# Gate columns and index weights with the tokens stationary, in a float32 two-block transformer kernel on Trainium2

## The reference, cut to what matters

```python
# first block: h is (256, 1024); the last 36 columns of w_in are the gates
z = h @ w_in
a_conv, q, kc_r, vc_r, ks, vs, kw, vw, g = jnp.split(z, splits, axis=-1)
gates = jax.nn.sigmoid(g).reshape(b, t, N_KV_HEADS, Q_PER_KV, N_BRANCH)   # 12 heads x 3 branches
out = gb[..., 0:1] * o_c + gb[..., 1:2] * o_s + gb[..., 2:3] * o_w

# second block: 8 index heads, w_i is (256, 8)
qa, ka, va, qb, kb, vb, qi, ki, wi, gate_a, gate_b = jnp.split(proj, split_at, axis=-1)
rel = jax.nn.relu(jnp.einsum('bqhd,bsd->bqhs', qi, k_i))
isc = jnp.einsum('bqhs,bqh->bqs', rel, wi) * idx_scale
logit = jnp.einsum('bqhd,bqkhd->bqhk', qa, kg) * scale     # "scores a", after a top-k by isc
```

## Time and profile before

| | before |
|---|---|
| runs | 737.31, 736.04, 737.00 us |
| median of the runs | 737.0 us |
| the profiled execution's own time | 736.97 us |
| its span, first to last instruction | 735.1 us |
| mean granted TensorE clock | 0.995 |
| busy: PE, PEld | 98%, 90% of the span |
| busy: DVE, ACT, POOL | 73%, 53%, 5% of the span |

### The profile page before, as it was taken

The page is one execution under the profiler, slowest core; times in us unless marked ns, Lnnn a source line. Parts: engine busy times, 40 slices in busy tenths (PEclk is TensorE's granted clock), DMA queues, the critical chain, the costliest instruction groups (busy, mean ns, idle before and its releaser), DMA issues.

```text
span 735.1 us, 13433 instructions
## 1 busy us (share of the span) xinstructions
PE 721.5 (98%) x5430; PEld 664.1 (90%) x5430; DVE 536.3 (73%) x935; ACT 388.9 (53%) x567; POOL 37.6 (5%) x53
## 2 busy tenths in 40 slices
PE   7999999999999999999999999999999999999996
PEld 7999987799999999988999989999888899999995
DVE  6798898676767777758569979995877885455554
ACT  7655999463344433447255457676446435445442
POOL 2700000000000000000532000000000000000000
PEclk9999999999999999999999999999999999999999
DMA  9746611678888778631554447454813774554511
GB/s 328 247 135 227 225 56 59 252 308 311 323 314 323 301 290 309 229 121 57 184 182 175 173 158 300 174 200 169 319 57 115 284 264 155 212 182 169 220 58 58
DMA packets 27024, 151.12 MB, mean 206 GB/s; under 512 B 3129, under 2 KB 7837, under 8 KB 9565
## 3 DMA queue, kind: packets, MB, share of 16 engines
q1 hardware_dynamic: 22620, 124.81, 46.7%
q10 hardware_dynamic: 3456, 25.17, 8.7%
q0 software_dynamic: 896, 0.43, 0.3%
HBM read 148.92 MB, written 1.05 MB: 204 GB/s over the span
## 4 chain that ended last, share of the span: by engine, by line
PE 84%; DVE 10%; ACT 3%; issue 1%; DMA 1%; SPq 0%; DVEq 0%; ACTq 0%
PE ps L464 25%; PE ps L465 24%; PE ps L466 24%; DVE w_lo L1820 3%; PE ps L860 2%; PE ps L598 1%; PE ps L622 1%; DVE misc L2333 1%; PE ps L582 1%; PE ps L1115 1%; DVE misc L2327 1%; DVE small L2332 1%; DMA raw<-rows_b 1%; PE ps L653 1%; PE ps L635 1%
## 5 line engine op out<-in xcount | busy, mean ns | idle before, releaser
L1820 DVE TENSOR_TENSOR w_lo<-raw,w_hi 128x2048 fp32r<-128x2048 f32 (+2 forms) x105 | 237.0, 2262 | 99.3 <-ACT w_hi L1294 99.1
L464 PE MATMUL ps<-h_hi,w_hi 128*128 128x256 f32 (+2 forms) x984 | 279.8, 284 | 0.0
L465 PE MATMUL ps<-h_lo,w_hi 128*128 128x256 f32 (+2 forms) x984 | 278.3, 283 | 0.0
L466 PE MATMUL ps<-h_hi,w_lo 128*128 128x256 f32 (+2 forms) x984 | 278.3, 283 | 0.0
L1294 ACT CAST w_hi<-raw 128x2048 fp32r<-128x2048 f32 (+2 forms) x105 | 197.0, 1888 | 49.4 <-PE ps L466 45.5
L464 PEld LDWEIGHTS ps<-h_hi,w_hi 128*128 128x128 f32 (+2 forms) x984 | 187.2, 190 | 2.5 <-issue 1.3
L465 PEld LDWEIGHTS ps<-h_lo,w_hi 128*128 128x128 f32 (+2 forms) x984 | 187.2, 190 | 1.1
L466 PEld LDWEIGHTS ps<-h_hi,w_lo 128*128 128x128 f32 (+2 forms) x984 | 187.2, 190 | 0.3
L464 PE MATMUL ps<-w_hi,mix_hi 128*128 128x512 f32 x248 | 97.6, 394 | 0.6 <-DVE small L1965 0.4
L465 PE MATMUL ps<-w_lo,mix_hi 128*128 128x512 f32 x248 | 96.8, 390 | 0.0
L466 PE MATMUL ps<-w_hi,mix_lo 128*128 128x512 f32 x248 | 96.5, 389 | 0.0
(11 more groups left out here) (326 smaller groups left out, 891.3 us busy)
## 6 DMA issues: line engine op xcount, KB each, us to landing
raw<-wts SPq DMA_DIRECT2D x109, 1024.0 KB, 4.8
ada<-w_ada ACTq DMA_DIRECT2D x24, 1024.0 KB, 5.2
alibi<-wts SPq DMA_DIRECT2D x2, 1024.0 KB, 6.0
fa_whole<-wts SPq DMA_DIRECT2D x2, 1024.0 KB, 5.8
resid<-x SPq DMA_DIRECT2D x2, 512.0 KB, 3.8
raw<-wts SPq DMA_DIRECT2D x2, 512.0 KB, 6.6
rows_ga<-rows_wide SPq DMA_DIRECT2D x1, 1024.0 KB, 8.4
out<-resid SPq DMA_DIRECT2D x4, 256.0 KB, 2.0
```

What stands on the lines that cost most here:

```text
L464: nc.tensor.matmul(o, lh, rh, start=start, stop=False)
L465: nc.tensor.matmul(o, lh, rl, start=False, stop=False)
L466: return nc.tensor.matmul(o, ll, rh, start=False, stop=stop)
L1820: V.tensor_tensor(w_lo[:, s % RING, 0:w], raw[:, n_of[name] % RAW, 0:w], w_hi[:, s % RING, 0:w].bitcast(F32), ALU.subtract).then_inc(w_rea ...
```

## The change

Both narrow projections are now made with the tokens stationary and 36 or 8 weight columns moving, once for each half of the tokens, so that they come out with tokens on the partitions. The copies to `gT` and `wiT` and the four transposes go. ACT reads the result where the transposes used to leave it. And four more slices of "sg0" stand ahead of `scores_a(0)`.

```diff
-            def narrow_tile(slot, o, a, n, cols):
+            def narrow_rows(slot, o, a, n, cols):
                 wh, wl = w3(slot, DC, DC * cols)
-                for k in range(DC):
-                    i = mm3(o, wh[:, k, a:a + n], wl[:, k, a:a + n], h_hi[:, k, :], h_lo[:, k, :], k == 0, k == DC - 1)
+                for m in range(2):
+                    ms = slice(m * P, (m + 1) * P)
+                    for k in range(DC):
+                        i = mm3(o(m), h_hi[:, k, ms], h_lo[:, k, ms], wh[:, k, a:a + n], wl[:, k, a:a + n], k == 0, k == DC - 1)
                 return i
...
-                narrow_tile(slot, ps[0:G_COLS, bank, 0:T], 0, G_COLS, G_COLS).then_inc(pe_tile, 1)
+                narrow_rows(slot, lambda m: ps[:, bank, T + m * HD:T + m * HD + G_COLS], 0, G_COLS, G_COLS).then_inc(pe_tile, 1)
...
-            def gate_turn():
-
-                pe.wait_ge(narrow_sb, 1)
-                for m in range(2):
-                    i = nc.tensor.transpose(ps[:, 7, T + m * HD:T + m * HD + G_COLS], gT[:, m * P:(m + 1) * P], ident[0:G_COLS, 0:G_COLS])
-                i.then_inc(narrow_ps, 1)
...
             cmp_values()
-            gate_turn()
             pe.wait_ge(lnv_ready, 1)
...
-            narrow_tile(slot, ps[0:NB_HEADS, bank, T:2 * T], P, NB_HEADS, IDX_COLS).then_inc(pe_tile, 1)
+            narrow_rows(slot, lambda m: ps[:, 7, m * NB_HEADS:(m + 1) * NB_HEADS], P, NB_HEADS, IDX_COLS).then_inc(pe_tile, 1)
...
             feature_2("qi0")
-            pe.wait_ge(narrow_sb, 2)
-            for m in range(2):
-                i = nc.tensor.transpose(ps[:, 7, m * NB_HEADS:(m + 1) * NB_HEADS], wiT[:, m * P:(m + 1) * P], ident[0:NB_HEADS, 0:NB_HEADS])
-            i.then_inc(narrow_ps, 1)
             feature_2("qi1")
...
-            gate_half(0, 0, 0, 3)
+            gate_half(0, 0, 0, 7)
             scores_a(0)
-            gate_half(0, 0, 3)
+            gate_half(0, 0, 7)
             gate_half(0, 1)
...
-                elif name == "g":
-                    nc.scalar.copy(gT, ps[0:G_COLS, bank, 0:T]).then_inc(narrow_sb, 1)
...
-                act.wait_ge(narrow_ps, 1)
+                act.wait_ge(pe_tile, s_idx["g"] + 1)
                 nc.scalar.activation(gates, ps[:, 7, T:T + 2 * HD] ... ACT.Sigmoid).then_inc(z_evac, 1)
...
-            copy_out(s_idx["g"])
             cmp_silu(1)
...
                 if name == "idx":
-                    nc.scalar.copy(wiT, ps[0:NB_HEADS, bank, T:2 * T]).then_inc(narrow_sb, 1)
+                    nc.scalar.copy(wi_s, ps[:, 7, 0:2 * NB_HEADS].rearrange("p (m h) -> p m h", m=2)).then_inc(wi_ready, 1)
                     nc.scalar.copy(kiT, ps[:, bank, 0:T]).then_inc(z_evac, 1)
...
-                if name == "qi0":
-                    act.wait_ge(narrow_ps, 2)
-                    nc.scalar.copy(wi_s, ps[:, 7, 0:2 * NB_HEADS].rearrange("p (m h) -> p m h", m=2)).then_inc(wi_ready, 1)
```

More of the change, by code:

```diff
@@ L181, in build @@
         pcmp = early[:, 2748:3516].rearrange("p (m h n) -> p m h n", m=2, h=NQ)
-        gT = early[0:G_COLS, 3516:3772]
-        wiT = misc[0:NB_HEADS, 1536:1792]
         probs = [soft[:, 0:768], soft[:, 768:1536], rows_ga[:, 0, 0:768], rows_ga[:, 1, 0:768]]
@@ L276, in build @@
         lnr_ready, lnrow_ps = sem("lnr_ready"), sem("lnrow_ps")
-        narrow_sb, narrow_ps, wi_ready = sem("narrow_sb"), sem("narrow_ps"), sem("wi_ready")
+        wi_ready = sem("wi_ready")
         sc_ps, sc_sb, pc_exp, pc_ready, pcT_ps, pcT_ready = (sem(n) for n in (
```

## The result

The changed kernel takes 748.58 us (median of 6 runs, 747.50 to 751.17) against 736.73 (6 runs, 736.04 to 737.44): ratio 1.0167, 95% interval 1.0145 to 1.0188. The sign was forecast, the size was not: +11.9 us instead of +4.5, far above the range. The profiled execution took 751.01 us (span 749.1), so its sum has to reach 751.01 - 736.97 = +14.0; it is one of the two slowest of the six, and its mean granted clock is 0.982 where the kernel before has 0.995. Over the six runs time and clock go together: 747.50 and 747.56 us at 0.990, 748.51 and 748.64 at 0.987 and 0.988, 751.01 and 751.17 at 0.982.

What follows compares the result with a forecast made beforehand. TensorE was taken to bound the kernel, with 84% of the span. Gate tile +2.48, index columns +2.53, gate transposes -0.10, index transposes -0.41 and scores 0 made +4.50: 736.97 to 741.5 us, 8-in-10 range 739.8 to 743.8.

Steps and rivals of the forecast that it cites:

- The pace of the loads, 0.111 us: Both narrow tiles: each of 48 matmuls takes as long as its 128-column load, 0.111 us, so 5.33 us a tile.
- The terms +2.48 and +2.53: Time TensorE loses in the gate tile (5.33 - 2.85) and in the index columns (5.33 - 2.80).
- forecast 2.53 - 0.41: Index columns: loss of 2.53 us in the tile, less 0.41 us for the index transposes that go.
- The bound by the row of L734: Narrow tiles at the compressed scores' load pace, 0.058 us each: both terms would be about -0.05 us.
- The rule of 1.2 GHz: Skill's load time, columns divided by 1.2 GHz, 107 ns for 128: the two tile terms together +4.6 instead of +5.0 us.
- The gate transposes, -0.10: Before cmp_scores: removing transposes of 0.24 us gains only 0.10, as the scores also wait for twelve DVE copies.
- The scores moved, 0: At scores_a(0): the 1.02 us wait moves behind the tile to L1101, shrinking to 0.7 to 0.8; counted 0, bounds -0.3 and +0.4.
- The sum without the clock, +4.5: Whole kernel: both tiles' losses less the transposes' gains, +4.50 us, giving 741.5; own bounds +4.0 and +6.0.
- rival (2): Narrow tiles: the clock falls to half for little streaming, one fall +1.7 us (743.2), two 744.9; chance 15%.
- loads go on without a pause: Narrow tiles: argument against a clock fall, that TensorE's loads never pause there; the skill doesn't say whether loads count.
- (1): Narrow tiles: loads overlap as with L734, 2.78 us a tile, so -0.6 us in all, 736.4; chance 10%.
- (3): Moved scores pay in full because the normalisation comes sooner: -1.0 us, so 740.5; chance 3%.

Runs made afterwards that it cites:

- e4: Changed kernel with 128 moving columns instead of 36 and 8 in the narrow tiles, extra products unused: 742.50 us, ratio 1.0068 to the kernel before.
- e9: From e2, index columns woven three thin matmuls behind three wide ones, through idx and the start of qi0: 739.64 us against 737.52 for the kernel before.
- e1: Kernel before with only the gate tile made tokens-stationary: 743.79 us against 737.53, ratio 1.0081.
- e3: Kernel before with only four more slices of sg0 ahead of scores_a(0): 737.09 us against 737.53, ratio 0.9996.
- e8: Kernel before, weights still stationary, hi and lo parts side by side in one operand, 16 matmuls a narrow tile instead of 24: 736.11 us against 737.32.
- e6: Changed kernel with each narrow tile cut into two halves, wide or other work between them: 746.76 us, ratio 1.0131 to the kernel before.
- e7: Changed kernel with six thin matmuls woven behind each three wide ones, gates in vs, index columns in idx: 750.91 us, ratio 1.0177 to the kernel before.
- e2: Kernel before with only the index columns made tokens-stationary: 742.31 us against 737.53, ratio 1.0065.
- e5: Changed kernel with 64 tokens stationary per half instead of 128, the other tokens left out: 737.99 us against 737.32 for the kernel before.

## Why the prediction was wrong

**The pace of the loads, 0.111 us: right.** At full clock the thin matmuls start 0.11 us apart in both tiles after, 0.113 in e4 with the streams widened, and 0.059 with half the columns stationary. The terms +2.48 and +2.53 stand: e9 measures the second, with the transposes gone, as +2.1 (forecast 2.53 - 0.41), and e1's one run without a fall gives +3.2 for the first (forecast +2.4), a single run. The bound by the row of L734 is -0.05 for the gate tile alone; for the index columns it is 2.80 - 2.80 = 0.

**The rule of 1.2 GHz, beside this.** The prediction weighed the rule of the Trainium skill (TensorE: Matmul & The Clock Gate, LDWEIGHTS), columns divided by 1.2 GHz. At full clock the trace is near the 107 ns that the prediction worked out from it, with 111; at half clock the loads start 0.213 us apart, so it does not hold there.

**The gate transposes, -0.10: borne out in its mechanism.** `cmp_scores` waits 0.2 us for the twelve copies after, as forecast. It starts at 88.29 instead of 80.88, 7.41 us late, where L598 ahead of the transposes' place is 7.51 late: 0.10 gained.

**The scores moved, 0: right.** The wait left L1053 and came back as 0.7 us at L1101, and e3's interval holds no difference; the profile after has 0.2 us of gain there, within the bounds.

**The sum without the clock, +4.5: right within half a microsecond.** e4 measures +5.0. The range that was given, 739.8 to 743.8, does not follow from the working: its own bounds of +4.0 and +6.0 give 741.0 to 743.0, and 743.2 and more with a fall; nothing in it leads to 739.8.

**The step that failed: the sum put the low clock at nothing, and rival (2) had its price and its chance wrong.** The forecast had a granted clock of 1.00 in both narrow tiles. Rival (2) said that the clock falls with so little streamed, and put it at "half of 3.4 us", +1.7 a fall, at 15%. The fall came in both tiles, and each lasted about 10 us. The 3.4 us were read from the earlier trace rows, a stretch at the start of the kernel that the engine left with dense matmuls ahead of it and where it also waits. Even there the price wasn't half of it: the first matmul of the dense work (L582) starts at 11.62, and the same one in the profile of e8, without a low clock at the start, at 10.86, only 0.76 us sooner. In the narrow tiles TensorE waits for nothing, and it is still in the thin tile when the clock falls: what is left of the 48 loads takes twice as long, so the sparse stretch grows by its own effect (5.3 us become 8.0 and 7.4), and the clock is given back some time behind its end. Priced from the profile after, the gate's fall costs 8.01 - 5.33 = 2.7 us in the tile, 1.0 in the convolution's mean and 1.3 in the scores, 5.0 in all; that of idx 7.39 - 5.33 = 2.1 and 2.6 in qi0's matmuls (its lateness grows from 12.02 at its start to 14.65 at its end), 4.7 in all. With the transposes that is 2.48 + 2.53 - 0.51 + 9.7 = +14.2, less 0.2 at the scores moved, for the profile's +14.0. The median run lost less: +11.9, of which e4 leaves about 7 to the clock.

The chance was wrong for a reason too. "Against: loads go on without a pause" took the loads for work that keeps the clock up, and e4 shows that with the same loads the array's streaming decides. A rival whose condition (hardly anything streamed, for 5.3 us) was written down in the forecast's own terms, and against which stood only an assumption, deserved, as judged now, about half the chance, and the range should have reached 745 with its own price and higher with the right one. Of the other rivals, (1) is refuted by the pace and (3) by the wait of 0.7 us.

**Open.** Why one of e6's four thin halves left the clock alone, why the same weave kept the clock up for the gates and not for the index columns (they differ in the columns moved and in their place), why falls also came beside short matmuls that the change doesn't touch (e4, e7), and why the low stretch at one and the same tile is 6.8 us in e2's profile and 10 in the one after, no run here tells. e1, e5 and the runs after show that a fall comes, and lasts, differently from run to run of one program.

## What to carry to other kernels

Before turning a product round so that its narrow side moves, count loads as well as columns: a tile of full loads with little to stream runs at the pace of the loads (0.11 us for 128 columns here), and what it saves in copies and transposes has to beat that on the critical path. Then ask what the granted clock will do with such a stretch, and price a fall by everything that runs until the clock is back, the rest of the stretch itself first. If thin matmuls can't be avoided, mix few of them with many wide ones (three index matmuls behind three wide ones held here, six didn't) and read the granted clock of that stretch in the profile. Better, see whether the narrow side can stay stationary in fewer, fuller matmuls, as in e8. And look at what the narrow tile was covering before making it shorter.

## What the runs showed of the hardware that was not expected

TensorE shown 100% busy by matmuls and loads lost its clock all the same: 2.00 of 2.00 us busy and 0.50 granted. Loads of 128 fp32r columns followed each other every 0.111 us at 2.4 GHz and every 0.213 at 1.2 GHz. More work was faster: with 128 moving columns in place of 36 and 8 the kernel lost 5.0 us instead of 11.9. And thin matmuls lowered the clock within 2.5 and 3.0 us in the profile after, without any idle time, where 1.3 us of idle time before the scores in e8 did not; in e7, 0.55 us of it before 64.43 and 1.61 us before 67.14 were followed by a fall at 67.7.
